# A two-block transformer on one core: seven more projection chunks of the last block as seven products, woven between the attention steps

## The reference

```python
h = _rmsnorm(x, g_mix)
rq, rk, rv, rg, nq, nk, nv, xq, gate_logits = jnp.split(h @ w_in, split_points, axis=-1)
y_ret = _retention_branch(rq, rk, rv, rg, ...)          # 4 heads, q and k rotated (rope)
y_na = _neighbourhood_attention(nq, nk, nv, rpb) @ w_na_o   # 8 heads of 64
y_xa = _memory_cross_attention(xq, _rmsnorm(mem, g_mem), w_mem_kv) @ w_xa_o  # 4 heads of 128
g_ret, g_na, g_xa = jnp.split(jax.nn.sigmoid(gate_logits), 3, axis=-1)
x = x + (g_ret * y_ret + g_na * y_na + g_xa * y_xa) @ w_out
x = x + _hierarchical_moe(_rmsnorm(x, g_ffn), ...)      # 16 experts
return _rmsnorm(x, g_final)
```

## Time and profile before

| | |
|---|---|
| median of 3 runs | 1748.38 us (1747.36 to 1749.61) |
| profiled execution, its own time | 1747.79 us |
| its span | 1746.1 us |
| TensorE busy | 1682.9 us (96%) |
| VectorE, ScalarE, GpSimd busy | 363.7, 290.3, 60.0 us |
| granted clock, mean | 0.996 |

### The profile page before, as it was taken

The page is one execution under the profiler, slowest core; times in us unless marked ns, Lnnn a source line. Parts: engine busy times, 40 slices in busy tenths (PEclk is TensorE's granted clock), DMA queues, the critical chain, the costliest instruction groups (busy, mean ns, idle before and its releaser), DMA issues.

```text
span 1746.1 us, 19240 instructions
## 1 busy us (share of the span) xinstructions
PE 1682.9 (96%) x8366; PEld 880.6 (50%) x8366; DVE 363.7 (21%) x820; ACT 290.3 (17%) x557; POOL 60.0 (3%) x90
## 2 busy tenths in 40 slices
PE   8999999989898999999999998999999999999997
PEld 7764443333333685634443333345744785556653
DVE  1341000000000325200000000031123762322222
ACT  2301101101010222101100010114131120222212
POOL 4000000000000101000000000032000000000000
PEclk9999999999999999999999999999999999999999
DMA  9878999999999935899999999997253435499996
GB/s 329 306 283 346 427 428 428 428 428 427 426 427 425 389 146 213 339 428 428 428 427 428 427 426 428 426 369 263 95 194 125 165 120 224 186 366 425 425 424 264
DMA packets 84804, 597.35 MB, mean 342 GB/s; under 512 B 5768, under 2 KB 14720, under 8 KB 51424
## 3 DMA queue, kind: packets, MB, share of 16 engines
q1 hardware_dynamic: 81152, 586.28, 82.6%
q0 software_dynamic: 3552, 9.65, 1.7%
HBM read 594.86 MB, written 1.05 MB: 341 GB/s over the span
## 4 chain that ended last, share of the span: by engine, by line
PE 65%; issue 18%; DMA 15%; DVE 1%; ACT 0%; POOL 0%; SPq 0%; POOLq 0%; DVEq 0%
PE psum L782 29%; PE psum L527 12%; DMA ring<-in_w_gate_dram 10%; PE psum L568 8%; DMA ring<-in_w_up_dram 4%; PE psum L583 3%; PE psum L767 3%; PE psum L817 2%; PE psum L575 2%; PE psum L631 1%; PE psum L728 1%; PE psum L644 1%; PE psum L659 1%; PE psum L838 1%; PE psum L519 1%
## 5 line engine op out<-in xcount | busy, mean ns | idle before, releaser
L782 PE MATMUL psum<-ring,xT 128*64 128x512 f32 (+1 forms) x2048 | 424.5, 562 | 34.9 <-DMA ring<-in_w_up_dram 16.3
L782 PEld LDWEIGHTS psum<-ring,xT 128*64 128x64 f32 x2048 | 146.2, 137 | 284.1 <-issue 248.1
L782 PE MATMUL psum<-ring,work 128*64 128x512 f32 x1056 | 234.6, 593 | 1.7 <-ACT work L1465 1.4
L527 PE MATMUL psum<-ring,xT 128*128 128x512 f32 x400 | 176.0, 593 | 0.0
L2039 DVE TENSOR_TENSOR work<-work,psum 128x512 f32<-128x512 f32 (+1 forms) x48 | 43.4, 905 | 634.7 <-PE psum L782 628.8
L782 PEld LDWEIGHTS psum<-ring,work 128*64 128x64 f32 x1056 | 75.1, 137 | 146.1 <-issue 139.0
L527 PEld LDWEIGHTS psum<-ring,xT 128*128 128x128 f32 x400 | 74.7, 190 | 88.6 <-issue 88.5
L568 PE MATMUL psum<-xT,ring 128*128 128x256 f32 x512 | 113.3, 380 | 0.7 <-DVE xT L1722 0.7
L1465 ACT COPY work<-psum 128x512 f32<-128x512 f32 (+1 forms) x48 | 24.7, 515 | 522.4 <-PE psum L838 522.4
L568 PEld LDWEIGHTS psum<-xT,ring 128*128 128x128 f32 x512 | 96.2, 190 | 14.5 <-DVE xT L1722 1.3
L782 PE MATMUL psum<-work,xT 128*64 128x512 f32 (+1 forms) x416 | 76.6, 513 | 0.0
(11 more groups left out here) (302 smaller groups left out, 1467.2 us busy)
## 6 DMA issues: line engine op xcount, KB each, us to landing
ring<-in_w_up_dram SPq DMA_DIRECT2D x53, 2048.0 KB, 23.8
ring<-in_w_down_dram SPq DMA_DIRECT2D x52, 2048.0 KB, 23.4
ring<-in_w_gate_dram SPq DMA_DIRECT2D x51, 2048.0 KB, 22.3
ring<-in_w_in_dram SPq DMA_DIRECT2D x16, 2048.0 KB, 10.3
ring<-in_w_exp_up_dram SPq DMA_DIRECT2D x16, 2048.0 KB, 18.5
ring<-in_w_exp_down_dram SPq DMA_DIRECT2D x10, 2048.0 KB, 20.2
work<-in_w_gate_dram SPq DMA_DIRECT2D x9, 2048.0 KB, 14.8
work<-in_w_exp_gate_dram SPq DMA_DIRECT2D x9, 2048.0 KB, 15.1
```

What stands on the lines that cost most here:

```text
L527: ins = pe.matmul(b[:, cols_at[0]:cols_at[1]], lhsT=lhsT(c), rhs=rhs(c), start=(c == order[0]), stop=(c == order[-1]))
L782: ins = pe.matmul(to[part * CAP:(part + 1) * CAP, 0:n], lhsT=lhsT, rhs=w[:, half * n:(half + 1) * n], start=first, stop=last)
```

## The change

Seven more chunks (two gates of the memory attention, nv, two gates of the neighbourhood attention, rq, rk) are computed as seven products. `open_seven` and `seven` are cut into single steps (`first`, `second`, `sixth`, `seventh`, `fifth`, `third`, `fourth`), which TensorE's program places between the attention steps. The first weight sum is formed in place, in the block that the first product reads, and waits for that product; the second weight sum goes to `prm`, the third in place. The token sums are made once, before the first of these chunks. rq and rk are first brought to SBUF, and the rotation reads them there. The gates of the two attentions are finished by corners and then passed through the sigmoid by whole rows of 1024. The keys' first half of the neighbourhood attention is made in two pieces around the last values of the memory attention. `keep_first` waits for the PSUM bank that it writes by its new number.

```diff
+            def sixth(m):
+                pe.wait_ge(S("token_sums"), 4)
+                pe.wait_ge(S("kept"), 3 * m + 1)
+                pe.wait_ge(S("weight_sums"), 4 * m + 2)
+                partial(chains[m], 0, token_sums[:, 1], weight_sum).then_inc(S("part"), 1)
+            def fifth(m):
+                pe.wait_ge(S("kept"), 3 * m + 2)
+                partial(chains[m], 0, token_sums[:, 0], block_of(sevens[m], 0, 0)).then_inc(S("part"), 1)
+            def third(m):
+                pe.wait_ge(S("kept"), 3 * m + 3)
+                partial(chains[m], 0, token_sums[:, 3], block_of(sevens[m], 1, 1)).then_inc(S("part"), 1)
...
             freed[n] = turned(as_cols(n), xT, DC, 4, "a", "xa"); n += 1
+            gate_0 = first(n)
             wait_made("xa")
             scores(att_x, 0, xa_q, xa_k)
-            w = as_cols(n)
-            tile(w, xT, DC, 512, 0, "a", "gate")
+            second(gate_0)
+            sixth_to_fifth(gate_0)
             scores(att_x, 1, xa_q, xa_k)
             turn_weights(att_x, 0)
-            freed[n] = tile(w, xT, DC, 512, 1, "a", "gate"); n += 1
+            third(gate_0)
+            gate_1 = first(n + 1)
+            freed[n] = fourth(gate_0); n += 1
+            second(gate_1)
             scores(att_x, 2, xa_q, xa_k)
             turn_weights(att_x, 1)
+            sixth_to_fifth(gate_1)
+            third(gate_1)
             scores(att_x, 3, xa_q, xa_k)
...
+            values_n = first(n)
             scores(att_n, 2, na_q, na_k)
             turn_weights(att_n, 1)
+            second(values_n)
+            sixth_to_fifth(values_n)
             scores(att_n, 3, na_q, na_k)
             turn_weights(att_n, 2)
+            third(values_n)
+            gate_0 = first(n + 1)
+            freed[n] = fourth(values_n); n += 1
+            second(gate_0)
             scores(att_n, 4, na_q, na_k)
             turn_weights(att_n, 3)
+            seven_made(values_n)
             values(att_n, 0, na_v)
+            sixth_to_fifth(gate_0)
+            third(gate_0)
             scores(att_n, 5, na_q, na_k)
             turn_weights(att_n, 4)
+            gate_1 = first(n + 1)
+            freed[n] = fourth(gate_0); n += 1
+            second(gate_1)
+            sixth(gate_1)
             scores(att_n, 6, na_q, na_k)
             turn_weights(att_n, 5)
             values(att_n, 2, na_v)
+            seventh(gate_1)
+            fifth(gate_1)
+            third(gate_1)
+            q = first(n + 1)
             scores(att_n, 7, na_q, na_k)
             turn_weights(att_n, 6)
+            freed[n] = fourth(gate_1); n += 1
+            second(q)
+            sixth(q)
+            seventh(q)
             turn_weights(att_n, 7)
             values(att_n, 4, na_v)
+            fifth(q)
+            third(q)
+            k = first(n + 2)
+            freed[n] = fourth(q); n += 1
             values(att_n, 6, na_v)
+            second(k)
...
             def sum_weights(m):
                 n = sevens[m]
-                t_1, t_2 = weight_sum[0][m], weight_sum[1]
-                dve.wait_ge(S(f"slot{n % RING}"), landed[n])
-                dve.tensor_tensor(t_1, block_of(n, 0, 1), block_of(n, 0, 0), ALU.subtract).then_inc(S("weight_sums"), 1)
+                dve.wait_ge(S("a_full"), opened[m])
+                dve.tensor_tensor(block_of(n, 0, 0), block_of(n, 0, 1), block_of(n, 0, 0), ALU.subtract).then_inc(S("weight_sums"), 1)
...
+            sum_tokens()
             oT = W(XA["oT"], 4, T)
+            sum_weights(GATE_X)
             peaks(att_x, 0)
+            first_corner(GATE_X)
             normal(att_x, 0)
+            other_corner(GATE_X, 3)
...
             output(oT[:, 1, :], True)
             normal(att_n, 6)
+            other_corner(GATE_N + 1, 3)
             peaks(att_n, 7, bias=near)
+            sum_weights(HEADS)
             normal(att_n, 7)
...
             variance(slice(0, 8), mv8[:, :, 1], GN_EPS)
-            first_corner(4)
-            sum_weights(5)
-            other_corner(4, 3)
+            sum_weights(GATE)
+            first_corner(GATE)
+            other_corner(GATE, 3)
+            sum_weights(GATE + 1)
...
+            def gated(gate, m):
+                act.wait_ge(S("corner"), 3 * m + 3)
+                for t in range(TC):
+                    act.activation(gate[:, t, :], gate[:, t, :], ACT.Sigmoid).then_inc(S("gate_a"), 1)
```

More of the change, by code:

```diff
@@ L584, in partial, with first @@
                 return ins
-            def open_seven(m, n):
+            def first(n):
+                m = len(sevens)
+                sevens.append(n)
                 chunk(n)
[L589 to L597, removed]
-                pe.wait_ge(S("kept"), 3 * m + 1)
+                chains.append(bank("a", by=(S("last_part"), m + 1)))
+                opened.append(taken["a"])
+                full("a", partial(chains[m], 0, tokens_of(0, 0), block_of(n, 0, 0), True))
+                return m
@@ new lines, in second, with seventh @@
+            def second(m):
+                full("v", partial(bank("v", by=(S("corner"), 3 * m + 1)), 0, tokens_of(0, 1), block_of(sevens[m], 1, 0), True))
+            def sixth(m):
+                pe.wait_ge(S("token_sums"), 4)
+                pe.wait_ge(S("kept"), 3 * m + 1)
+                pe.wait_ge(S("weight_sums"), 4 * m + 2)
+                partial(chains[m], 0, token_sums[:, 1], weight_sum).then_inc(S("part"), 1)
+            def seventh(m):
+                corners.append(bank("a", by=(S("corner"), 3 * m + 3)))
+                cornered.append(taken["a"])
@@ L599, in seven @@
                 pe.wait_ge(S("weight_sums"), 4 * m + 3)
[L600 to L603, removed]
+                full("a", partial(corners[m], 0, token_sums[:, 2], block_of(sevens[m], 0, 1), True))
+            def fifth(m):
                 pe.wait_ge(S("kept"), 3 * m + 2)
-                partial(chain, 0, token_sums[:, 0], weight_sum[0][m]).then_inc(S("part"), 1)
@@ L612, in seven, with sixth_to_fifth, seven_made @@
                 return S("part"), 4 * m + 4
+            def sixth_to_fifth(m):
+                sixth(m)
+                seventh(m)
+                fifth(m)
+            def seven_made(m):
+                pe.wait_ge(S("corner"), 3 * m + 3)
+                pe.wait_ge(S("last_part"), m + 1)
             def as_cols(n, at=0, width=512):
@@ L1250, in _ @@
-            freed[n] = seven(2, n, lambda: open_seven(3, n + 1)); n += 1
-            freed[n] = seven(3, n, heads_turned); n += 1
+            sixth_to_fifth(k)
+            wait_made("joined")
+            values_0 = first(n + 1)
+            third(k)
+            freed[n] = fourth(k); n += 1
+            second(values_0)
+            sixth_to_fifth(values_0)
+            values_1 = first(n + 1)
+            third(values_0)
+            freed[n] = fourth(values_0); n += 1
+            second(values_1)
@@ L1252, in _ @@
+            sixth_to_fifth(values_1)
+            gate_0 = first(n + 1)
+            third(values_1)
+            freed[n] = fourth(values_1); n += 1
+            second(gate_0)
+            sixth_to_fifth(gate_0)
+            gate_1 = first(n + 1)
+            third(gate_0)
+            freed[n] = fourth(gate_0); n += 1
+            second(gate_1)
+            sixth_to_fifth(gate_1)
+            heads_turned()
+            third(gate_1)
+            freed[n] = fourth(gate_1); n += 1
             wait_made("rqk")
-            pe.wait_ge(S("corner"), 3 * 2)
@@ L1271, in _ @@
             yT, comb = W(RET["yT"], DC, T), W(W_COMB, TC, D)
-            open_seven(4, n)
-            freed[n] = seven(4, n, lambda: open_seven(5, n + 1)); n += 1
-            freed[n] = seven(5, n, lambda: turn(W(RET["y"], TC, D), DC, "oT", "gn", rings="v")); n += 1
+            gate_0 = first(n)
+            second(gate_0)
+            sixth_to_fifth(gate_0)
+            gate_1 = first(n + 1)
+            third(gate_0)
+            freed[n] = fourth(gate_0); n += 1
+            second(gate_1)
+            sixth_to_fifth(gate_1)
+            turn(W(RET["y"], TC, D), DC, "oT", "gn", rings="v")
+            third(gate_1)
+            freed[n] = fourth(gate_1); n += 1
             wait_made("oT")
@@ new lines, in first_corner, with other_corner @@
+            def first_corner(m):
+                n, to, b = sevens[m], seven_to[m][0], bank()
+                dve.wait_ge(S("kept"), 3 * m + 1)
+                dve.tensor_tensor(to, b[:, 0:256], to, ALU.add).then_inc(S("corner"), 1)
+                dve.wait_ge(S("weight_sums"), 4 * m + 3)
+                dve.tensor_tensor(block_of(n, 1, 0), block_of(n, 1, 0), weight_sum, ALU.subtract).then_inc(S("weight_sums"), 1)
+            def other_corner(m, at):
+                if at == 3:
+                    dve.wait_ge(S("a_full"), cornered[m])
+                else:
+                    dve.wait_ge(S("part"), 4 * m + 4)
+                dve.wait_ge(S("kept"), 3 * m + at)
+                to = seven_to[m][at]
```

(1 more changed line is left out.)

304 lines of the change are left out of this document (164 added, 140 removed).

## The result

Four runs of the changed kernel gave 1757.74 to 1759.9 us, median 1759.13; four of the kernel before had a median of 1748.99. The ratio is 1.0059 (95% interval 1.0046 to 1.0071): 0.6% slower. The forecast was 1746.5 with a range up to 1749.6, and a chance of 0.09 for slower.

What follows compares the result with a forecast made beforehand. TensorE alone was taken to set the pace; -11.6 - 0.96 + 4.55 + 2.2 + 0.3 + 3.6 = -1.9 us gave a median of 1746.5 us, with 8 in 10 for 1742.7 to 1749.6.

Steps and rivals of the forecast that it cites:

- What I cost at nothing: Part copies, corners, token sums, rotation from SBUF, whole-row sigmoids, reordered key projection and a PSUM bank wait: no cost.
- the margins of the walk: Attention stretch, VectorE's and TensorE's queues: elsewhere 0.3 to 3 us of margin for in-place sums, attention weights in time.
- The last two gate chunks: In-place sums queue behind y's group statistics on VectorE and hold sixth: 3.6 us, nothing more behind.
- Columns: Seven chunks as seven products, 56 instructions of 256 columns each: 1.65 us saved per chunk, 11.6 in all.
- First wait: Before the first scores, the first gate chunk's first product covers TensorE's wait for ScalarE: 0.96 us gained.
- Exposed evictions: Six places where TensorE waits for ScalarE's chain bank copy: five at 0.74, one at 0.85, sum 4.55 us.
- Late sums in the query-head chunk: In the query-head chunk the sums queue behind the peaks of head pair 7: 0.3 us late.
- Port conflict: First chunk: VectorE's sums and GpSimd's mask additions shut each other out; 2.2 us with 0.25 of own lateness.
- Rival (a): No port conflict for VectorE's sums: -3.9 us, 1744.5; chance 0.16.
- Rival (c): VectorE falls behind in the neighbourhood attention and stalls TensorE: about 1752 us; chance 0.07.
- Rival (b): Sums before the last gates do not hold TensorE, or most evictions are half covered: gain 5.5, 1742.9; chance 0.12.
- (d): Stalls a little larger, 0.3 to 0.5 us at each of eight places: 1747 to 1750; chance 0.20.

Runs made afterwards that it cites:

- experiment 1: Changed kernel with ScalarE's four exponentials of the decay matrices moved behind its next three copies: 1751.49 us, ratio 1.0017 to the kernel before.
- experiment 4: Kernel before with only VectorE's decay block moved behind the next two corners: 1757.16 us, ratio 1.0049 to the kernel before.
- experiment 2: Changed kernel with the last two gate chunks' first sums in places of their own and VectorE's earlier order there: 1751.31 us, ratio 1.0015.
- experiment 7: Changed kernel with matmuls nobody reads put in its two long waits, five and three of them: 1754.39 us, ratio 1.003 to the kernel before.
- experiment 8: Changed kernel with GpSimd's mask additions held back behind the memory attention, a single execution for its trace: 1757.11 us.
- Experiment 5: Changed kernel with the edits of experiment 1 and experiment 2, and TensorE's order changed at the six exposed copies: 1740.5 us, ratio 0.9951.

## Why the prediction was wrong

**The step that failed: the moved decay block, which the sum has no term for.** "What I cost at nothing" and the margins of the walk speak of VectorE's queue, and of TensorE waiting for VectorE. The move of the decay block is not among what it costs at nothing, and no reason is given for leaving it out. That ScalarE waits for the block, and holds a copy that TensorE needs, was not read. Nothing new had to be known for it: the order in ScalarE's queue stands in the code, and the margin in the trace of before was 1.16 us against 7.6 us by which the block moved. It costs 5.2 us of wait and 2.9 of clock, 8.1 in all; experiment 1 gives back 7.6, and experiment 4 makes the kernel before 8.5 slower by this move alone. Without it the changed kernel is 0.17% slower than before (experiment 1), within what I had called no change.

**The last two gate chunks: right in mechanism, mis-sized.** The term was 3.6, and sixth was held 3.64 us by the sums, as worked out. The stretch lost 7.3, and experiment 2 gives back 7.8. Two parts were missing: the clock behind the idle (1.6, and 0.15 in the next group), and the wait of fifth in the last chunk (1.76). "So nothing more comes" was checked for the turning of y only. The gate's sigmoid was not followed back to VectorE, where the last corner stands behind the normalisation, and the normalisation behind the second chunk's in-place sums. Nor was the copy behind the sigmoid followed forward to TensorE.

**The clock.** No term had it; a wait was priced at its length. Over both long waits that left out 2.9 + 1.6 = 4.5 us, and experiment 7, where the waits remain, is 4.7 faster. Behind an idle of 1.8 us no such loss shows: the product at 1452.39 takes 1.83 to the next start (1454.22), at a granted clock of 1.00. The price is not one number: behind the same idle of 5.2 us 1.5 us were lost in experiment 2, 2.5 in experiment 4, 2.6 in experiment 8 and 2.9 in the changed kernel. No run shows what decides between them. The Trainium skill, TensorE: Matmul & The Clock Gate, section "HAM oscillation — how this bites in real kernels", says that what follows a long wait of TensorE runs at half the clock until it is released again; the trace agrees, with 0.50 and 0.52 behind the two long waits.

**The other terms held.**
- Columns: the seven chunks run at 56 instructions of 0.216, and the neighbourhood stretch gains 2.45, where its four chunks less the stalls forecast in it (4 x 0.74 + 0.85 + 0.3) made 4 x 1.65 - 4.1 = 2.5.
- First wait: the first product covers it, and the first scores follow that product with no gap (1187.67 + 1.73 = 1189.40).
- Exposed evictions: six, at the places named. A row for one: third would start at 1213.54, started at 1214.16, and its next group at 1215.99, so it cost 0.72, where 0.74 was taken. The sixth was 0.73 where 0.85 was taken. Sum 4.3 for 4.55. Experiment 5 agrees with places and size together.
- Late sums in the query-head chunk: 0.24 for 0.3. Sixth was wanted at 1314.76 + 3.45 = 1318.21, when VectorE's second sum (1317.08 to 1318.31) was not done, and started at 1318.45.
- Port conflict: 1.35 where the forecast had 2.2 less the own lateness of 0.25, so 1.95; that lateness is 0.24 in experiment 8. Right in kind, since experiment 8 takes it away. It was too high here because the first sum was not held: GpSimd's additions began 0.2 us behind it (1189.80 and 1189.60), where the forecast had them begin half a microsecond ahead. After that a sum ended every 1.9 us, as forecast. In experiments 1 and 7, where the first sum took 1.55, the conflict cost 1.7. Rival (a) is excluded.
- Rival (c), VectorE falling behind in the neighbourhood attention: no turning or sixth there waits for it beyond the 0.24 above. Rival (b) is excluded by the two waits seen, and (d) by terms that came out at or below their forecast up to the join.

So up to the join the forecast came out within 0.5 us, and "slower" arose from a mechanism that was none of the rivals. Put together: the forecast difference was -1.9; with 8.1 for the decay block, 3.7 for clock and second wait in the last gates, and 0.5 less in the first stretch it is +9.4, which is what the changed stretches of the two traces differ by. Measured in medians is 1759.13 - 1748.99 = +10.1; the rest is within the scatter of the unchanged stretches.

## What to carry to other kernels

When a block of one engine's program is moved, list who waits for its result in every other queue and what stands behind that wait there; the instruction that stalls the bounding engine may be neither the moved one nor one that reads its result. Forming a sum in place ties it to the product that reads the block first, so where a queue is busy at that moment it needs a place of its own. Both repairs cost no work and turned 0.6% slower into 0.3% faster; with the exposed copies covered and the mask additions moved as well it was 0.6% faster. A wait of the bounding engine can cost more than its length: here 1.5 to 2.9 us more behind 5.2, and 1.6 to 1.8 more behind 3.6.

## What the runs showed of the hardware that was not expected

- After TensorE had stood for 5.2 us its granted clock was 0.50 (1.2 GHz) for 3.5 us and 0.60 in the mean of the next 2.8, at a cost of 2.9 us; behind the same idle in experiment 2 the second group was at full rate and the cost 1.5. After 3.6 us idle it was 0.52 for 3.2 us, at a cost of 1.6. Matmuls that nobody reads, put into the idle, removed the cost (experiment 7).
- Two-input sums of VectorE beside GpSimd's additions take 1.90 to 2.01 us instead of 1.22, and GpSimd 1.45 instead of 0.97 each (11.60 and 7.77 for eight). The Trainium skill, SBUF — State Buffer, section "SBUF: two separate sides", says that the two exclude each other for such operations, and the traces agree: while both are at it, one GpSimd addition starts every 1.84 to 1.94 us and a sum ends every 1.9. The other way round, GpSimd's one operation in the fourth stage, beside which the late sums now run, took 2.58 us where the earlier trace rows has 1.67.
